# Expert blocks of a hybrid decoder step: the third weight is issued from ScalarE's queue

## The reference, cut to what matters

```
x <- LN(ALPHA*x + Mix(x));  x <- LN(ALPHA*x + HMoE(x))

gates = (top-1 of 4 groups, then top-2 of the 4 experts in it)     # 16 experts per layer
h = silu(x @ w1[e]) * (x @ w3[e])                                  # 1024 -> 256
y = sum over the token's two experts of gate * (h @ w2[e])         # 256 -> 1024
```

## Time and profile before

| what | value |
|---|---|
| median of 3 runs | 1831.86 us (1819.35 to 1833.63) |
| the profiled execution's own time | 1819.13 us |
| its span, first to last instruction | 1817.2 us |
| mean granted TensorE clock | 0.893 of full speed |
| TensorE (PE) busy | 1518.7 us, 84% |
| VectorE (DVE) busy | 623.7 us, 34% |
| ScalarE (ACT) busy | 337.4 us, 19% |
| GpSimd (POOL) busy | 127.5 us, 7% |
| moved by DMA | 317.68 MB, mean 175 GB/s |

### The profile page before, as it was taken

One profiled execution on the slowest core, in us unless ns is written; L12 is line 12 of the kernel. 1 busy time (PEld: TensorE's weight loads), 2 busy tenths in 40 slices (PEclk: granted clock), 3 DMA queues, 4 the chain that ended last, 5 costly groups with the idle time before them and its releaser, 6 DMA issues.

```text
span 1817.2 us, 22736 instructions
## 1 busy us (share of the span) xinstructions
PE 1518.7 (84%) x9044; PEld 1008.2 (55%) x9044; DVE 623.7 (34%) x1354; ACT 337.4 (19%) x677; POOL 127.5 (7%) x118
## 2 busy tenths in 40 slices
PE   5999988778889199999099999887897965999990
PEld 3465455554545188887044655654564444888870
DVE  1141245745654400000502404466476350000005
ACT  1000023323301022221210000233141011222211
POOL 0001001000000220000200010101000005000002
PEclk9999998868889599999599999888696976999995
DMA  7129344448140668887431302454464035888854
GB/s 278 46 79 307 96 126 149 157 98 171 47 141 4 258 260 337 337 336 275 161 111 47 121 6 99 113 174 132 126 149 142 2 139 208 355 339 330 343 229 165
DMA packets 135909, 317.68 MB, mean 175 GB/s; under 512 B 51348, under 2 KB 81556, under 8 KB 114708
## 3 DMA queue, kind: packets, MB, share of 16 engines
q1 hardware_dynamic: 106640, 187.44, 29.3%
q0 software_dynamic: 12672, 86.51, 15.6%
q10 hardware_dynamic: 16516, 42.63, 6.2%
HBM read 267.35 MB, written 49.19 MB: 174 GB/s over the span
## 4 chain that ended last, share of the span: by engine, by line
PE 25%; issue 15%; DVE 7%; POOL 1%; ACT 1%; DMA 1%; ACTq 0%; POOLq 0%; DVEq 0%
PE ps L1605 10%; PE ps L1887 3%; DVE ring L987 1%; PE ps L1706 1%; DVE z L987 1%; PE ps L1608 1%; PE ps L1688 1%; PE ps L1669 1%; POOL x L724 1%; PE ps L1651 1%; PE ps L1635 1%; DVE xT L987 1%; PE ps L1818 1%; PE ps L1829 1%; PE ps L1530 0%
## 5 line engine op out<-in xcount | busy, mean ns | idle before, releaser
L1605 PE MATMUL ps<-ring,xT 128*128 128x512 f32 (+1 forms) x896 | 363.2, 565 | 1.3 <-ACT xT L742 1.3
L1932 PEld LDWEIGHTS ps<-z,ring 128*128 128x128 f32 x2432 | 295.4, 198 | 19.2 <-issue 17.0
L1932 PE MATMUL ps<-z,ring 128*128 128x128 f32 x2432 | 295.7, 283 | 1.4 <-ACT z L742 1.4
L1605 PEld LDWEIGHTS ps<-ring,xT 128*128 128x128 f32 x896 | 168.8, 190 | 185.2 <-issue 180.3
L742 ACT ACTIVATE ring<-ps 128x512 f32<-128x512 f32 (+2 forms) x186 | 95.8, 540 | 380.4 <-PE ps L1706 196.5
L987 DVE TENSOR_TENSOR z<-ps,vbuf 128x512 f32<-128x512 f32 (+3 forms) x84 | 47.6, 570 | 325.4 <-PE ps L1605 292.6
L742 ACT ACTIVATE z<-ps 128x512 f32<-128x512 f32 (+1 forms) x152 | 78.8, 542 | 411.6 <-PE ps L1932 222.1
L1942 PE MATMUL ps<-ring,z 128*128 128x512 f32 x304 | 140.4, 605 | 6.3 <-DVE z L987 2.0
L987 DVE TENSOR_TENSOR z<-z,ps 128x256 f32<-128x256 f32 x38 | 16.0, 421 | 322.6 <-ACT z L742 322.6
L1887 PE MATMUL ps<-ring,xT 128*128 128x512 f32 x256 | 114.7, 608 | 2.4 <-DMA ring<-in_w_out 1.9
L1706 PE MATMUL ps<-tab,kbuf 128*128 128x128 f32 x512 | 93.0, 311 | 10.8 <-DMA kbuf<-in_cache_k,idx_k 5.5
(11 more groups left out here) (248 smaller groups left out, 1553.2 us busy)
## 6 DMA issues: line engine op xcount, KB each, us to landing
ring<-in_w SPq DMA_DIRECT2D x114, 1024.0 KB, 7.3
ring<-in_w_in SPq DMA_DIRECT2D x12, 2048.0 KB, 8.6
z<-expert_rows ACTq DMA_DIRECT2D x38, 512.0 KB, 5.1
expert_rows<-z ACTq DMA_DIRECT2D x38, 512.0 KB, 4.4
expert_rows<-zero SPq DMA_DIRECT2D x1, 12288.0 KB, 53.2
ring<-in_w_out SPq DMA_DIRECT2D x4, 2048.0 KB, 10.8
vbuf<-in_b_in SPq DMA_DIRECT2D x2, 1670.0 KB, 10.5
ring<-in_w_in SPq DMA_DIRECT2D x2, 1072.0 KB, 5.7
```

The costliest lines, as they stand in the source:

```text
L1605: m = mm(ps[0:n, i % 4, 0:w], xTv[:, k, t * P:t * P + n], slab[at % 3][:, k, 0:w], start=(k == 0), stop=(k == KD - 1))
L1932: m = mm(ps[:, 2 + s, at:at + BLOCK], w13[s][:, w, q, c::2], xgT[s][:, q, :], start=(q == 0), stop=(q == KD - 1))
```

## The change

SP's loop no longer issues `w3` for the blocks two ahead; it issues `w1` alone at the place where it issued both, and `w2` as before. The first two blocks of each layer, loaded ahead of the loop, still get `w1` and `w3` from SP. ScalarE, in each of the 34 blocks with `more`, reads the expert of block `k + 2` from the plan into a register, waits for `h_ps` as before, and now issues the DMA of `w3` between that wait and Silu. The number of DMAs, their sizes and the semaphores that they raise stay the same.

```diff
+                    def load_w1(e, s):
+                        sp.dma_start(w13[s][:, 0], d["w1"][e].rearrange("o (p k) f -> p (o k) f", p=P)).then_inc(w13_in[s], 16)
+
                     def load_w13(e, s):
-                        sp.dma_start(w13[s][:, 0], d["w1"][e].rearrange("o (p k) f -> p (o k) f", p=P)).then_inc(w13_in[s], 16)
+                        load_w1(e, s)
                         sp.dma_start(w13[s][:, 1], d["w3"][e].rearrange("o (p k) f -> p (o k) f", p=P)).then_inc(w13_in[s], 16)
...
                         for s in range(2):
                             sp.wait_ge(h_ps, i * 2 + (s - 1))
-                            load_w13(es[s], s)
+                            load_w1(es[s], s)
...
                     def act_block(i, k, s, more, turn):
                         if more:
                             load_block(k + 2, s)
+                            e = bass.ds(layer * EXPERTS + act.value_load(plan[0:1, bass.ds(k + 2, 1)], min_val=0, max_val=EXPERTS - 1), 1)
                         act.wait_ge(h_ps, k + 1)
+                        if more:
+                            act.dma_start(w13[s][:, 1], d["w3"][e].rearrange("o (p k) f -> p (o k) f", p=P)).then_inc((w13_in0, w13_in1)[s], 16)
                         f(sil[s], ps[:, 2 + s, 0:2 * BLOCK], ACT.Silu).then_inc(sil_sb, 1)
```

## The result

The changed kernel took 1871.01 us (median of 4 runs, 1865.58 to 1875.49), the kernel before 1825.61 us beside it: a ratio of 1.0246, 95% interval 1.0183 to 1.0308. A later set of runs gave 1863.58 against 1820.78, ratio 1.0230 (1.0176 to 1.0284). By these two ratios the change makes the kernel 2.3 to 2.5% slower.

A forecast was written before the change was run, and what follows sets the result against it. The prediction took TensorE's own order of h, transposes, y to bound the expert stages. Issues (17.7 us) plus table loads (21.8) add 39.5 us to the 1831.86 median, giving 1871.4 us, 2.2% slower; range 1846 to 1884.

The forecast's parts named there:

- the sum: Both expert stages: 17.7 us for issues plus 21.8 for table loads, 39.5 us added; bounds 33.4 to 42.3.
- The chain ends last, nothing covers: Between h and y, Silu and multiplication end after the transposes; y starts 0.97 us after Silu, so any delay moves y.
- The issue of `w3`, 0.52 us: On ScalarE between h and Silu, 34 blocks: Silu 0.52 us late (0.34 to 0.55), 17.7 us in all.
- The table load, 1.28 us in 17 blocks: On ScalarE in slot 0, the load moves behind the DMA issue, right before Silu: 21.8 us in all.
- The clock is no term: TensorE's busy share falls from 98% to about 91%, without lowering its granted clock; no cost.
- the prediction's own sign: In the expert stages, a granted clock below 0.99 would show the prediction wrong.
- The read of the plan, zero: On ScalarE ahead of the wait for `h_ps`: 34 register loads fit in idle time, cost zero; uncovered, 9 us.
- No gain from queues: SP's loop loses one issue per block and `w2` goes out some 0.4 us sooner, worth nothing while TensorE does not wait.
- The load off the path: Rival: the table load runs ahead of the DMA, so only the issue costs, 17.7 us, 1849.6 us; chance 0.12.
- The draining load: Rival: up to 1.50 us of ScalarE idling moves with each load, up to 25.5 us more, 1896.9; chance 0.05.
- Weights that had been late: Rival: weights were late in ordinary runs; freeing them regains at most 12.7 us: 1858.7 (chance 0.10), or 1836.9 and faster (0.05).

The follow-up runs named there:

- the kernel with the load ahead: Changed kernel plus a one-column Silu ahead of the wait for `h_ps` in slot 0, so the table load runs early; 1848.41 us, ratio 1.0124 to the kernel before.
- the kernel with `w3` behind Silu: Changed kernel with two statements swapped, Silu first, then the issue of `w3`, still from ScalarE; 1831.48 us, ratio 1.0001 to the kernel before.
- the read behind the wait: Changed kernel with ScalarE's read of the plan moved from ahead of the wait for `h_ps` to behind it; 1900.76 us, ratio 1.0463 to the kernel before.

## Why the prediction was right, and where its sum was off

The time came out at the forecast, 1871.01 against 1871, and the direction and cause are as stated. The agreement to the microsecond is partly luck. The forecast stood on a median of 1831.86; with one more run that is 1825.61, so the change cost 45.4 us by the medians, and 48.3 in the profiled stages, against 39.5. Both are above the 42.3 that the sum allowed at most: a base too high by 6 us hid a cost too low by 6. Term by term:

- **The chain ends last, nothing covers.** Right. y followed Silu by 0.96 to 0.97 us in every block of the changed kernel; lengthening the chain by 0.1 to 2.5 us cost that much, shortening it by 0.12 gained that.
- **The issue of `w3`, 0.52 us.** 0.56 measured (0.60 from h to Silu, less 0.04), just over the upper bound of 0.55. In the block of slot 1 above the issue starts 1685.60 - 1685.42 = 0.18 us after h, takes 0.37, and Silu starts 0.05 later; the prediction had 0.17, 0.35 and 0.03. 34 x 0.56 = 19.0 us instead of 17.7.
- **The table load, 1.28 us in 17 blocks.** Right, and the larger part. Slot 0 is later than slot 1 by 1.92 - 0.60 = 1.32 us, the load and 0.04 around it; 22.4 us instead of 21.8. The 1.38 us of drain that the Trainium skill, page "ScalarE: Activation LUTs", section "What ACT_TABLE_LOAD costs", adds to a load is absent here too: the load at 1671.93 ends at 1673.21, and Silu starts at 1673.23.
- **"The clock is no term."** This is the step that failed, by the prediction's own sign: the granted clock of the earlier stage is 0.97, not 0.99. The busy share did fall to 91% (223.80 of 246.43 us), as it said. But that such a share keeps the clock was read from one stretch, 78% busy at 1.00, and the next 20 us of the same trace, 16.11 of 20 or 81% busy, were granted 0.78:

```profile
280.00:300.00 20.00, 16.11 (x141) 10.78 (x141) 9.22 (x16) 5.82 (x10) 1.87 (x2) 0.78 0.44 160
```

The busy share of a stretch did not tell the clock. In the changed kernel it fell behind gaps of 2.0 us, 4 times in one profile and 6 in the other, and each time y took 1.70 us longer: 6.8 and 10.2 us.

- **The sum.** 19.0 + 22.4 + 6.8 = 48.2, measured 48.3; for the second profile 19.0 + 22.4 + 10.2 = 51.6, measured 51.5.
- **The read of the plan, zero.** Right: with the issue behind Silu it costs nothing, without its cover 0.60 us a block. On ScalarE it is dearer than on SP, 0.44 against 0.27 us in the median, still inside the idle time.
- **No gain from queues.** Right: with the path untouched, `w3` on ScalarE's queue gives 1.0001.
- **The rivals.** The load off the path is the kernel with the load ahead, +20.0 us in the stages against the 17.7 forecast for that case. The draining load did not show: from the end of the issue at 1671.90 to Silu at 1673.23 there is the load and 0.05 us. Weights that had been late would have made the kernel with `w3` behind Silu, which takes `w3` out of SP's queue at no cost, faster than before; its ratio is 1.0001, and TensorE names no DMA among its waits in the changed stages.

## What to carry to other kernels

Before putting an issue on an engine, measure the interval from the event to the consumer with and without the cover (here the last block of a layer, which has no transposes): if it is the same, nothing is free there. The same issue one statement later cost nothing.

## What the runs showed of the hardware

TensorE's granted clock can fall behind a single gap in a stage that is 91% busy. Of the 17 blocks of slot 0 in each kernel, with the same matmuls between the gaps, none had a drop to 1.2 GHz behind gaps of 0.73 and 1.49 us; behind 2.00 us 4 and 6 had one, behind 2.48 us 5, behind 2.61 us 9. Blocks of slot 1, with gaps of 0.22 to 1.27 us, had none. A longer gap also makes the stage's busy share lower, and these kernels do not tell the two apart; why some gaps of one length are followed by a drop and others not was not tried.

Two DMA issues in a row on ScalarE take 0.83 us, and the second adds 0.46 to 0.48 us to whatever is behind them. Where SP and ScalarE issue upon the same event, the one at 1671.49 and the other at 1671.55 us in the changed kernel, ScalarE's issue of `w3` took 0.365 us in the median; with the read behind the wait it starts 0.6 us later and took 0.339. What makes these 0.03 us was not tried.
